# Transposing the normed rows with DMAs from SBUF to SBUF instead of matmuls, in a two-layer decoder step on eight cores

## What is computed

```python
def layer(x, past_pool, start_pos, norm_g, w_in, w_pool, pool_scale, v_norm_g, w_s, b_s, w_out):
    h = rmsnorm(x, norm_g)                       # x * rsqrt(mean(x*x) + EPS) * norm_g
    proj = jnp.einsum('btd,de->bte', h, w_in)    # 1024 -> 2560: a_in, a_gate, u, v, b_gate
    ctx = jnp.concatenate([past_pool, a_in], axis=1)
    a_out = pool_mix(ctx, ..., w_pool, pool_scale) * jax.nn.silu(a_gate)
    vn = rmsnorm(v per head, v_norm_g)
    b_out = chunk_mix(u, vn, w_s, b_s) * jax.nn.silu(b_gate)
    y = x + jnp.einsum('bte,ed->btd', jnp.concatenate([a_out, b_out], axis=-1), w_out)
```

## Time and profile before

| | us |
|---|---|
| time, median of 3 runs (489.38 to 489.92) | 489.78 |
| the profiled execution, its own time | 489.68 |
| its span on the slowest core (core 4) | 488.1 |
| PE busy | 458.0 (94% of the span) |
| DVE busy | 318.1 (65%) |
| ACT busy | 178.8 (37%) |
| POOL busy | 116.9 (24%) |

### The profile page before, as it was taken

How to read it: one execution, slowest core, us unless ns; L and a number is a source line. 1 busy time by engine, 2 the same in 40 slices (tenths; PEclk the granted TensorE clock), 3 DMA queues, 4 the chain that set the end, 5 groups by cost and what they waited for, 6 DMA issues and landing times.

```text
span 488.1 us, 7755 instructions; the slowest of 8 cores (484.3 to 488.1 us)
## 1 busy us (share of the span) xinstructions
PE 458.0 (94%) x2428; PEld 213.5 (44%) x2428; DVE 318.1 (65%) x593; ACT 178.8 (37%) x296; POOL 116.9 (24%) x208
## 2 busy tenths in 40 slices
PE   3679999999899999999999999999999999999991
PEld 1334444444444454444544445444454445444440
DVE  1656657479857587766776768467574657766665
ACT  3324341391036502258132740035501471333044
POOL 8142013610063101351027200043101510270000
PEclk9989999999999999999999999999999999999997
DMA  7999970699049401630045000000000000220013
GB/s 199 181 172 183 213 212 2 108 156 170 10 55 168 82 0 44 202 104 1 1 157 188 3 4 1 0 3 28 5 1 1 0 1 1 87 109 3 1 44 129
DMA packets 10499, 36.97 MB, mean 76 GB/s; under 512 B 1822, under 2 KB 2334, under 8 KB 8892
## 3 DMA queue, kind: packets, MB, share of 16 engines
q0 software_dynamic: 4048, 19.20, 21.5%
q1 hardware_dynamic: 5548, 16.12, 10.9%
q10 hardware_dynamic: 864, 1.16, 0.7%
HBM read 42.19 MB, written 10.09 MB: 107 GB/s over the span
## 4 chain that ended last, share of the span: by engine, by line
PE 82%; DVE 6%; ACT 3%; issue 3%; POOL 2%; DMA 2%; ACTq 0%; DVEq 0%; POOLq 0%
PE pF L517 55%; PE pF L1007 19%; PE pT L501 3%; DMA xg<-x 2%; PE pF L980 2%; PE pF L737 1%; PE pF L943 1%; ACT vscr L775 1%; DVE Tt L568 1%; DVE xg L1013 1%; DVE hT L505 1%; DVE ss L594 1%; POOL ss L443 1%; DVE vn_sb L606 1%; PE pF L971 1%
## 5 line engine op out<-in xcount | busy, mean ns | idle before, releaser
L517 PE MATMUL pF<-hT,win 128*128 128x512 bf16 x1024 | 232.8, 381 | 2.5 <-DVE vn_sb L606 2.5
L517 PEld LDWEIGHTS pF<-hT,win 128*128 128x128 bf16 x1024 | 99.3, 98 | 119.4 <-issue 6.5
L1007 PE MATMUL pF<-wout,mix 128*128 128x512 bf16 x512 | 114.8, 379 | 0.3 <-DVE mix L962 0.2
L1007 PEld LDWEIGHTS pF<-wout,mix 128*128 128x128 bf16 x512 | 48.9, 98 | 56.9 <-issue 2.3
L1013 DVE TENSOR_TENSOR xg<-pF,xg 128x512 f32<-128x512 f32 x64 | 44.1, 688 | 30.0 <-PE pF L1007 29.3
L517 PE MATMUL pF<-win,hT 128*128 128x512 bf16 x272 | 60.7, 379 | 1.0 <-DVE hT L505 1.0
L479 ACT ACTIVATE vscr<-xg 128x1024 bf16<-128x1024 f32 x40 | 42.2, 1056 | 45.1 <-DVE xg L1013 38.7
L591 ACT ACTIVATE vscr<-pF 128x512 f32<-128x512 f32 x32 | 19.1, 597 | 97.2 <-PE pF L517 82.1
L491 ACT ACTIVATE hb<-xg,ssx 128x1024 bf16<-128x1024 f32 x28 | 31.9, 1143 | 53.5 <-PE pT L501 48.2
L442 POOL TENSOR_SCALAR ssx<-ssx 128x1 f32<-128x1 f32 (+3 forms) x24 | 6.0, 248 | 166.3 <-ACT vscr L479 166.0
L442 POOL TENSOR_SCALAR ss<-ss 128x4 f32<-128x4 f32 (+1 forms) x34 | 10.5, 308 | 140.6 <-DVE ss L594 140.2
(11 more groups left out here) (106 smaller groups left out, 359.8 us busy)
## 6 DMA issues: line engine op xcount, KB each, us to landing
win<-win_h POOLq DMA_DIRECT2D x8, 1024.0 KB, 27.6
y<-xg SPq DMA_DIRECT2D x12, 512.0 KB, 3.0
xg<-x SPq DMA_DIRECT2D x9, 512.0 KB, 5.2
wout<-wout_h POOLq DMA_DIRECT2D x4, 1024.0 KB, 32.6
xg<-x POOLq DMA_DIRECT2D x7, 512.0 KB, 45.6
win<-win_h POOLq DMA_DIRECT2D x4, 256.0 KB, 13.6
win<-win_h POOLq DMA_DIRECT2D x2, 512.0 KB, 18.8
y<-hT ACTq DMA_DIRECT2D x4, 256.0 KB, 2.6
```

Of the source, the lines that this page charges most:

```text
L517: r = h.matmul(out=out_ap, lhsT=lhsT(k), rhs=rhs(k), start=(k == 0), stop=(k == 7))
L1007: r = h.matmul(out=pf[:, :], lhsT=mix[:, k, i * 128:(i + 1) * 128], rhs=wout[l][:, hf, k, :], start=(k == 0), stop=(k == 7))
```

## The change

`norm_dt(i)` takes the place of PE's half of `norm_tr`: a DMA started from ACT's queue transposes tile i from `hb` straight into `hT` (bf16, 128x1024). `norm_g(l, i0, n)` takes the place of DVE's half: 8 `tensor_scalar` instructions multiply `hT` in place by the norm weights, one for each block of 128 model columns, for one tile (128 elements a partition) or for two (256). The first item's own rows still go through `norm_tr`. The loads are moved: the rest of the staging data goes to the end of POOL's first batch, the sample rows get a semaphore of their own on SP's queue, and `load_second` moves from item 1 (after the V projection) to item 0 (after BGATE).

```diff
-        stage(stg[:, 640:1152], wsk_d[:, 640:1152], buf("wsf1"), deps=[wop["wout0_1"]])
+        stage(stg[:, 640:1152], wsk_d[:, 640:1152], buf("wsf1"), eng=POOL)
         for l in range(2):
-            stage(st_sb[l].rearrange("p r j -> p (r j)"), stp_d[l], buf(f"st_sb{l}"))
-        ldma(xs_sb, xs_d[:, :], buf("xs"))
+            stage(st_sb[l].rearrange("p r j -> p (r j)"), stp_d[l], buf(f"st_sb{l}"), eng=POOL)
+        S.emit(SP, lambda h: h.dma_start(out=xs_sb, in_=xs_d[:, :]), writes=[buf("xs")], dma="xsl", deps=[wop["wout0_1"]])
...
+        def norm_dt(i):
+
+            j = i % NHB
+            S.emit(ACT, lambda h: h.dma_start_transpose(out=hT[:, :, i * 128:(i + 1) * 128], in_=hb[:, j, :]),
+                   reads=[buf(f"hb{j}")], writes=[buf(f"hT{i}")], dma=f"tr{i}")
+
+        def norm_g(l, i0, n=1):
+            hbufs = [buf(f"hT{i}") for i in range(i0, i0 + n)]
+
+            def f(h):
+                r = None
+                for k in range(8):
+                    c = slice(i0 * 128, (i0 + n) * 128)
+                    r = h.tensor_scalar(out=hT[:, k, c], in0=hT[:, k, c], scalar1=gT[:, l, k:k + 1], scalar2=None, op0=ALU.mult)
+                return r
+            S.emit(DVE, f, reads=hbufs + [buf(f"gT{l}")], writes=hbufs)
...
-                hk["bg"] = [lambda: prep_ws(0)]
+                hk["bg"] = [lambda: prep_ws(0), load_second]
             if n == 1:
-                hk["v"] = [load_second]
...
+                norm_dt(0)
+                norm_dt(1)
                 for i in range(TPG):
                     out_mm(i, 0)
...
                 nrm.scale(2)
+                norm_dt(2)
...
                 out_mm(0, 1)
-                norm_tr(*nx, 0)
+                norm_g(nx[1], 0)
                 nrm.scale(3)
-                norm_tr(*nx, 1)
+                norm_dt(3)
                 out_mm(1, 1)
                 out_mm(2, 1)
-                norm_tr(*nx, 2)
+                norm_g(nx[1], 1)
+                norm_g(nx[1], 2)
                 out_mm(3, 1)
-                norm_tr(*nx, 3)
+                norm_g(nx[1], 3)
                 return
             if nx is not None:
-                norm_tr(*nx, 0)
+                for i in range(NHB):
+                    norm_dt(i)
                 nrm.scale(3)
-                norm_tr(*nx, 1)
+                norm_dt(3)
...
-                if i < 2:
-                    norm_tr(*nx, 2 + i)
+                if i == 1:
+                    norm_g(nx[1], 0)
+                if i == 2:
+                    norm_g(nx[1], 1, 2)
+                if i == 3:
+                    norm_g(nx[1], 3)
```

## The result

The changed kernel takes **516.05 us** (median of 4 runs, 515.41 to 518.44), the kernel before 489.58 us beside it (4 runs, 489.19 to 489.92): a ratio of 1.055, 95% interval 1.0515 to 1.0585. It is slower by 26.5 us, where 478.0 was forecast with a range up to 493. The range misses it by 23 us.

The account below looks back on a forecast made before the run. PE was taken as the bound, with 82% of the chain. From 489.7 us, 15.6 removed, 1.4 added for DVE waits and 2.5 for item 0 gave 478.0 us, range 472 to 493.

Parts of the forecast that it names:

- what is removed: PE loses line 501's transposes, 13.4 us for 28 tiles, and two waits in item 1, 2.2 us: 15.6 us.
- Removal and two waits: Item 1: transposes of 2.11 us leave PE's chain, and two waits for DVE go, 0.94 + 1.24 = 2.2 us.
- the cost and the waits: DVE's small multiplications take 1.6 us a tile; the fourth V projection waits 0.7 us in items 3 and 6, 1.4 lost.
- The price of a DMA: A transposing DMA lands in 2.6 us, like a plain 256 KB store on ACT's queue; no cost outside item 0.
- Rival A: Transposing DMAs slow and serial, PE waits at every item's head: 643 us at 10.4 us each, 506 at 5.5; chance 0.17.
- Item 0: Transposes under memory load, landing priced at 7.3 us: 2.5 us lost, between 0.8 overlapped and 13.0 one after another.
- Rival B: Item 0 alone has serial transposes under load, losing 13.0 us in place of 2.5: 488.5 us; chance 0.09.
- The moved loads at zero: POOL starts the second layer's loads in item 0, where it has nothing else to do; priced at no cost.
- -15.6 + 1.4 + 2.5: Whole sum: 15.6 us removed from PE, 1.4 lost to DVE in items 3 and 6, 2.5 lost in item 0.
- the estimated 10.5 us a tile: Skill page's 1309 ns a block for eight blocks in a row by DMA; the sum would then be rival A's.

Follow-up runs that it names:

- item 0 on PE: Changed kernel, loads still moved, but item 0's four tiles transposed by PE as before, items 1 to 6 by DMA: 479.03 us, ratio 0.9798 to the kernel before.
- the norm weights one tile earlier: Kernel with item 0's tiles on PE, DVE's norm-weight multiplications of later items each one output tile earlier: 478.81 us, ratio 0.9772.
- smaller packets: Changed kernel, each block of the second layer's input weights loaded by four DMAs of 256 KB instead of one of 1 MB: 515.68 us, ratio 1.0526.
- the loads after item 0's transposes: Changed kernel, second layer's loads started only when item 0's four transposing DMAs have landed: 485.92 us, ratio 0.993.
- two blocks early: Changed kernel, only two of five weight blocks loaded in item 0, the other three and the pooling weights in item 1: 501.76 us, one execution.

## Why the prediction was wrong

- **What bounds the kernel, and what is removed: right in kind, a little too large.** PE's busy time fell by 13 us. A plain item, 5 or 6, is shorter by 1.48 us and not 1.79. With item 0 on PE, item 1 is shorter by 4.5 us; of this the moved loads alone give 1.1 (55.1 in place of 56.3 us), which I had at zero. Removal and two waits were priced at 2.1 + 2.2 = 4.3 there. Where the missing 0.3 us of a plain item stays, no run tells.
- **DVE: right about the cost and the waits.** Eight multiplications of 128 elements take 1.39 us (1.6 forecast), of 256 elements 1.65 (2.2). The fourth V projection waits 0.28 us at the head of item 4, and two wait 0.28 us each at the head of item 7, where 0.7 each was forecast. Counted by items, item 4 gains 0.4 us in place of the 1.5 of a plain item and item 7 loses 0.8, together 1.8 us against the 1.4 of the sum. That the total is near is partly luck: with the norm weights one tile earlier both waits are gone, item 7 is 1.1 us shorter, and item 4 stays at 65.4 us. What item 4 lacks is therefore not shown to be DVE's backlog.
- **The price of a DMA: right outside item 0.** 3.2 us against 2.6. Its start keeps ACT's queue for 1.25 to 1.3 us (2.1 at most), not 0.5; the prediction named this as not priced, and outside item 0 it cost nothing that shows. Rival A (0.17) has the sign, but not the mechanism: outside item 0 the landings took 3.1 to 4.9 us, median 3.2, and with item 0 on PE nothing waited for one.
- **Item 0: the step that failed.** I gave it 2.5 us of wait with an upper bound of 13.0, so with the 1.79 removed there item 1 was to begin 0.7 us later. PE waited 36.4 us, and item 1 began 32.9 us later. (Where the working says "the third scaling waits for the landing of tile 0", it is the fourth, that of tile 3.) The working took the landing of a 44 KB copy under load (7.3 us) as the price of a transpose under load. That row has the right queue and the wrong quantity: beside a full queue the price goes by packets, and a transpose has 1056 of them. No row of before shows this number, so the bound should have come from the worst the load could do. That was readable: the first batch keeps the engines busy to about 72 us in the earlier trace rows, and 5 blocks of 1 MB and `wpool` behind it take some 31 us more at the 172 GB/s of the same group, to 103 us. A first V projection that can't begin before 103 is 27 us late, by which the sum would be 502 us, with the other sign.
- **Rival B named the right place, mis-sized.** "Item 0 alone, serial under load" was priced by the same 7.3 us a tile. The row of ACT's queue shows a second thing that was mis-sized: the second start ends only at 103.83, 4.0 us before the first tile lands at 107.80, so square, root and scaling of tiles 2 and 3 stand behind it for 41 us. In this kernel they then cost PE next to nothing more (0.22 us), because the first tile is as late; with smaller packets the second and third tile cost 12.8 + 8.4 us.
- **The moved loads at zero: wrong as a sum of parts.** They cost nothing alone (0.9983), and the transposes cost nothing beyond forecast where there are no loads (0.9798). I had written that the weights fill the gap of 0.01 DMA share at 72 to 87 us in the earlier trace rows, and that item 0's transposes run there, but I priced this only by the row of 44 KB, and the loads themselves at nothing.
- **The clock, a small addition.** The changed kernel's windows over the hole and behind it (length; busy us of PE, PEld, DVE, ACT, POOL; PEclk, DMA share, GB/s):

```profile
72.00:82.00 10.00, 1.06 (x5) 0.29 (x3) 0.00 (x0) 0.00 (x0) 0.00 (x0) 0.77 1.05 192
82.00:92.00 10.00, 0.00 (x0) 0.00 (x0) 0.00 (x0) 0.00 (x0) 0.00 (x0) 0.50 1.04 171
...
112.00:115.00 3.00, 2.78 (x8) 1.04 (x8) 1.69 (x8) 1.11 (x2) 0.00 (x0) 0.50 0.43 83
115.00:117.00 2.00, 2.00 (x11) 0.94 (x10) 1.25 (x8) 0.00 (x0) 0.00 (x0) 1.00 0.04 7
```

PE stood idle, the granted clock fell from 1.00 (2.4 GHz) to 0.50 (1.2 GHz), and was back at 1.00 in the window that begins 5.6 us after PE had resumed at 109.44. In between PE worked at half speed. This is why item 1 gained 1.8 us here and 4.5 with item 0 on PE: 2.7 us more that the hole cost. It does not take a hole of 36 us: behind the 5.6 us of the loads after item 0's transposes item 1 takes the same 54.4 us.

The whole of it: -15.6 + 1.4 + 2.5 = -11.7 forecast. Without item 0's transposes the spans differ by 488.1 - 477.2 = 10.9 us. With them they differ by 25.6 us the other way. Nearly all of the 36.5 us between these two is item 0's: item 1 begins at 109.4 in place of 75.5 us (34.0), and its slow clock costs 2.7.

## What to carry to other kernels

Before a load is moved into a gap of the DMA engines, list what else the same change wants from them there, and price the two together. For a transfer of many small packets, count packets and not bytes: next to a full queue it goes at the pace of that queue's packets, and the bound of its landing is the time until that queue is empty. Here its first packet was 4 to 5 us late as well. A transposing DMA is a good trade for PE time only where the queues are empty, and in the stretch where weights are still coming the transposes belong on PE.

## What the runs showed of the hardware

- A DMA transpose of 128x1024 bf16 from SBUF to SBUF is 1056 packets, nearly all of 256 bytes, and lands in 3.2 us with nothing beside it; a plain store of as many bytes took 2.6 us in the earlier trace rows. The Trainium skill's page Advanced Engine Details and Errata, section X-Bar Transpose (TRN2), has transposes as fast as plain DMAs; with nothing beside it the trace comes near that. What a plain DMA of this size takes beside a full queue no run shows. The page VectorE: DVE Perf Modes, section The three transpose paths, has 1309 ns for one 128x128 block; here eight blocks took 3.2 us, so the estimated 10.5 us a tile that it gave is not what happens.
- Beside POOL's queue of 7.2 KB packets the same transpose passes at 24 packets a microsecond, beside 1.8 KB packets at 66, and alone at some 760 (2046 packets in 38.3% of the 7 us from 108 to 115).
- The start of a transposing DMA keeps ACT for 1.25 to 1.3 us (2.1 at most) with no load beside it, and for up to 40 us while another transpose is still passing under load:

```profile
L513 ACTq DMA_TRANSPOSE hT<-hb x28: 1247/1277/40086, 62.1 to 440.7; - x28
```

This is the changed kernel's line of starts: count, then min, median and max in ns. The start held all that ACT had to do next. The second start ended 3 to 5 us before the first transpose landed in the changed kernel and in those with two blocks early and with smaller packets; what releases it no run shows.

- With POOL's queue full, the first packet of a transpose came 4 to 5 us after its start (62.09 to 66.5, 64.97 to over 69), with no other queue at work about 1.1 us after it.
- In the kernel with the loads after item 0's transposes the granted clock was 0.50 (1.2 GHz) from 80 to 84 us behind a wait of PE of 5.6 us, and the item behind it took 54.4 us, as behind the wait of 36.4 us; with a granted clock of 1.00 it takes 51.7.
